# Norm sums behind the attention output and the gated projection: two reduced-precision products in place of one fp32 product

## The reference

```python
for i in range(DEPTH):
    hn = rms_norm(h, norm_mix_pre[i])
    m = deltanet_stickbreak_mixer(hn, ...) if i % 2 == 0 else s5_mixer(hn, ...)
    h = h + rms_norm(m, norm_mix_post[i])
    hn = rms_norm(h, norm_ffn_pre[i])
    f = swiglu_ffn(hn, ffn_w_gate[i], ffn_w_up[i], ffn_w_down[i])
    h = h + rms_norm(f, norm_ffn_post[i])

def rms_norm(x, w):
    return x * lax.rsqrt(jnp.mean(x * x, axis=-1, keepdims=True) + EPS) * w
```

## Time and profile before

| | us |
|---|---|
| median of three runs | 2797.24 |
| lowest, highest | 2795.65, 2801.64 |
| profiled execution | 2792.69 |
| its span, first to last instruction | 2790.9 |
| TensorE matmul busy in it | 2707.2 |
| VectorE busy | 1243.0 |
| GpSimd busy | 1008.4 |
| ScalarE busy | 615.2 |

### The profile page before, as it was taken

One profiled execution on the slowest core, in us unless ns is written; L12 is line 12 of the kernel. 1 busy time (PEld: TensorE's weight loads), 2 busy tenths in 40 slices (PEclk: granted clock), 3 DMA queues, 4 the chain that ended last, 5 costly groups with the idle time before them and its releaser, 6 DMA issues.

```text
span 2790.9 us, 44901 instructions
## 1 busy us (share of the span) xinstructions
PE 2707.2 (97%) x18169; PEld 2577.4 (92%) x18169; DVE 1243.0 (45%) x2137; ACT 615.2 (22%) x1085; POOL 1008.4 (36%) x462
## 2 busy tenths in 40 slices
PE   8999899989999999999999989899999999999997
PEld 7999788867899999999999878799999999999997
DVE  5665566565145444444442446710532322222234
ACT  4231333365241000000000332311410000000002
POOL 6444110033444444444442414152444444444440
PEclk9999999999999999999999999999999999999999
DMA  5236221121231222222222159841331111111102
GB/s 166 93 109 137 84 73 51 58 74 38 70 107 50 78 85 85 85 85 85 85 85 79 51 142 248 246 121 33 106 106 46 45 45 45 45 45 45 46 31 81
DMA packets 158150, 236.51 MB, mean 85 GB/s; under 512 B 57808, under 2 KB 120528, under 8 KB 155856
## 3 DMA queue, kind: packets, MB, share of 16 engines
q1 hardware_dynamic: 53552, 137.11, 16.0%
q10 hardware_dynamic: 104480, 97.71, 12.0%
HBM read 174.89 MB, written 64.09 MB: 86 GB/s over the span
## 4 chain that ended last, share of the span: by engine, by line
issue 37%; PE 36%; POOL 14%; DMA 6%; DVE 3%; ACT 1%; ACTq 1%; SPq 1%; POOLq 0%; DVEq 0%
POOL w_hi L736 9%; PE psum L778 8%; PE psum L779 7%; PE psum L780 7%; POOL w_lo L739 5%; DMA stage<-wstream 5%; PE psum L860 2%; PE psum L1260 2%; DVE area L2291 2%; PE psum L1234 1%; PE psum L1082 1%; PE psum L1103 1%; DVE area L2198 1%; PE psum L1247 1%; DMA area<-s 0%
## 5 line engine op out<-in xcount | busy, mean ns | idle before, releaser
L778 PE MATMUL psum<-x_hi,w_hi 128*128 128x344 f32 (+2 forms) x3456 | 1127.0, 326 | 5.0 <-POOL w_lo L739 3.9
L779 PE MATMUL psum<-x_lo,w_hi 128*128 128x344 f32 (+2 forms) x3456 | 1107.9, 321 | 0.0
L780 PE MATMUL psum<-x_hi,w_lo 128*128 128x344 f32 (+2 forms) x3456 | 1106.5, 320 | 0.0
L736 POOL TENSOR_TENSOR w_hi<-stage,const 128x1024 fp32r<-128x1024 f32 x193 | 478.7, 2480 | 1564.6 <-PE psum L780 1414.0
L778 PEld LDWEIGHTS psum<-x_hi,w_hi 128*128 128x128 f32 x3456 | 651.5, 189 | 16.8 <-POOL w_lo L739 5.4
L779 PEld LDWEIGHTS psum<-x_lo,w_hi 128*128 128x128 f32 x3456 | 651.4, 188 | 3.5 <-issue 1.7
L780 PEld LDWEIGHTS psum<-x_hi,w_lo 128*128 128x128 f32 x3456 | 650.8, 188 | 0.0
L739 POOL TENSOR_TENSOR w_lo<-stage,w_hi 128x1024 fp32r<-128x1024 f32 x193 | 485.3, 2515 | 15.1
L2680 DVE TENSOR_TENSOR area<-area,psum 128x344 f32<-128x344 f32 (+2 forms) x132 | 67.7, 513 | 648.4 <-ACT area L1937 648.4
L778 PE MATMUL psum<-act_hi,w_hi 128*128 128x344 f32 (+2 forms) x1056 | 342.8, 325 | 11.8 <-DVE area L2693 7.3
L780 PE MATMUL psum<-act_hi,w_lo 128*128 128x344 f32 (+2 forms) x1056 | 338.0, 320 | 0.0
(11 more groups left out here) (235 smaller groups left out, 2208.2 us busy)
## 6 DMA issues: line engine op xcount, KB each, us to landing
stage<-wstream SPq DMA_DIRECT2D x193, 512.0 KB, 3.5
s_set<-area ACTq DMA_DIRECT2D x8, 1860.0 KB, 7.8
proj<-area ACTq DMA_DIRECT2D x20, 520.0 KB, 2.7
area<-proj ACTq DMA_DIRECT2D x36, 256.0 KB, 3.7
resid<-area ACTq DMA_DIRECT2D x6, 1376.0 KB, 5.8
area<-resid ACTq DMA_DIRECT2D x6, 1376.0 KB, 10.2
area<-s SPq DMA_DIRECT2D x8, 1024.0 KB, 12.2
area<-s SPq DMA_DIRECT2D x8, 836.0 KB, 10.9
```

What stands on the lines that cost most here:

```text
L736: pool.tensor_tensor(per_block(w_hi[:, slot, :]), src, ones_block, ALU.mult).then_inc(high_split, 1)
L778: mm(out[:, 0:n], w_hi[:, slot, wk], hi[:, xk, a:a + n], start=first, stop=False)
L779: mm(out[:, 0:n], w_hi[:, slot, wk], lo[:, xk, a:a + n], start=False, stop=False)
L780: return mm(out[:, 0:n], w_lo[:, slot, wk], hi[:, xk, a:a + n], start=False, stop=last)
```

## The change

In rounds 1 and 3 a sum is no longer an fp32 product. ScalarE, after squaring a half, waits for the square and copies it, rounded to fp32r, into `x_hi`, in the columns of the cut itself, which no product reads any more. VectorE subtracts that from the square into the same columns of `x_lo` (new function `square_low`). TensorE runs eight fp32r products of a rounded matrix of ones with `x_hi` and eight with `x_lo`, accumulated in the same bank. It waits for each half of either. The ones are rounded once by ScalarE at the start. `square_low` is set into VectorE's list at twelve places.

```diff
+        def split_sums(r):
+            return r in (1, 3)
+        def split_event(r, c, m):
+            return 6 * (r // 2) + 2 * c + m
+        ones_r = sb("ones_r", [P, P], F32R)
...
+                if split_sums(r):
+                    a = cuts_of(r)[c][0]
+                    pe.wait_ge(ones_ready, 1)
+                    for x, done in ((x_hi, nm_sq_high), (x_lo, nm_sq_low)):
+                        for k in range(KT):
+                            if k % 4 == 0:
+                                pe.wait_ge(done, 2 * split_event(r, c, m) + k // 4 + 1)
+                            last = mm(sums[:, 0:n], ones_r[:], x[:, k, a:a + n], start=x is x_hi and k == 0,
+                                      stop=x is x_lo and k == KT - 1)
+                    last.then_inc(nm_sum, 1)
+                    return
...
                     A(sq[half][:, :, 0:n], x[:, ks], ACT.Square).then_inc(nm_square, 1)
+                    if split_sums(r):
+                        act.wait_ge(nm_square, 2 * e + half + 1)
+                        A(x_hi[:, ks, a:a + n], sq[half][:, :, 0:n], ACT.Copy).then_inc(nm_sq_high, 1)
...
             norm_load(0, 0)
             act.wait_ge(eps_ready, 3)
+            act.wait_ge(params_loaded, 32)
+            A(ones_r[:], ones, ACT.Copy).then_inc(ones_ready, 1)
...
+            def square_low(r, c, m):
+                a, n = cuts_of(r)[c]
+                for half in range(2):
+                    ks = slice(4 * half, 4 * half + 4)
+                    dve.wait_ge(nm_sq_high, 2 * split_event(r, c, m) + half + 1)
+                    V.tensor_tensor(x_lo[:, ks, a:a + n], sq_halves[half][:, :, 0:n], x_hi[:, ks, a:a + n].bitcast(F32), sub
+                                    ).then_inc(nm_sq_low, 1)
...
             for c in range(2):
+                square_low(1, c, 0)
                 norm_post(1, c)
+                square_low(1, c, 1)
                 norm_pre(1, c)
                 norm_low(1, c)
+            square_low(1, 2, 0)
...
                 norm_post(r, 2)
                 step(0, 1)
+                square_low(r, 2, 1)
                 step(0, 2)
...
-            glu_product(range(19))
+            glu_product(range(18))
+            square_low(3, 0, 0)
+            glu_product((18,))
             norm_post(3, 0)
             glu_product((19,))
+            square_low(3, 0, 1)
             norm_pre(3, 0)
             glu_product((20,))
             norm_low(3, 0)
+            square_low(3, 1, 0)
             glu_product((21,))
             norm_post(3, 1)
             glu_product((22,))
+            square_low(3, 1, 1)
             norm_pre(3, 1)
             glu_product((23,))
+            square_low(3, 2, 0)
             norm_low(3, 1)
             ffn(1, 3)
```

More of the change, by code:

```diff
@@ L471, in trunk @@
         nm_sum = sem("nm_sum")
+        nm_sq_high = sem("nm_sq_high")
+        nm_sq_low = sem("nm_sq_low")
+        ones_ready = sem("ones_ready")
         nm_stored = [sem(f"nm_stored{i}") for i in range(2)]
```

## The result

The kernel after takes 2812.61 us (2807.96 to 2818.05), the one before, on the same chip, 2795.65 (2793.70 to 2801.64): a ratio of 1.0049 [1.0032, 1.0067], or 13.7 us slower. The direction was right and the size was not.

A forecast was written before the change was run, and what follows sets the result against it. TensorE, busy 97% of the span, was taken as the bound: shorter sums would save 22 us if nothing waited, but late input makes layer 0 +4.2 and layer 1 +3.1, +7.3 on 2797.24, so 2804.5 us; range 2793 to 2810.

The forecast's parts named there:

- sum three: Second cut, first norm: input late beside GpSimd's splits; lasts 5.75 us against 4.36, loss 1.4 in each layer.
- the walk of the lock: VectorE's subtractions and GpSimd's splits wait for each other in turn; in the second cut's first norm, loss 1.4 us.
- Sum one: First cut, first norm: input ready in time, 16 products take 2.56 us instead of 4.46, gain 1.9.
- Sum two: First cut, second norm: input late though GpSimd is idle; lasts 4.6 us against 4.46, loss 0.2.
- Sum four: Second cut, second norm: split, subtraction, split, subtraction; lasts 7.6 us against 4.4, loss 3.2 in each layer.
- rival A: Second cut, second norm, each layer: the other order, loss 1.35 us instead of 3.2; total 2801.8; chance 0.25.
- sum five: Third cut, first norm: 6.8 us instead of 4.4 in layer 0; in layer 1 input is ready, 2.5 us.
- T3 to T5: From the first product behind the fourth sum to that behind the sixth: 37.3 us in layer 0, 35.5 in layer 1.
- B: At the subtractions beside splits, GpSimd doesn't hold VectorE: -4.0 us, total 2793.2; chance 0.14.
- C: At all changed sums, TensorE's own work decides and all input is hidden: -22 us, total 2775; chance 0.04.
- E: The ones product runs at today's rate for each of 16 products: another 4.4 us per sum, over +50; chance 0.03.
- D: Later links in the chains slip too: +12 us, total 2809; chance 0.11.

The follow-up runs named there:

- the first experiment: Against the kernel before, only the first sum of each of the two places is two rounded products, the other ten stay fp32: 2788.24 us, ratio 0.9976.

## Why the prediction was right in direction and short in size

**The step that failed first: sum three.** The prediction took the first square of the second cut at T1 + 7.1 and low parts clear of the splits, as before. It counted the two copies on ScalarE for the evacuations behind them, and left out the store's issue, which stands in the same queue. With it the pre norm starts 1.0 later, the first square at T1 + 7.9 in layer 0 (777.87), and low parts, subtractions and splits meet one after the other. Sum three took 9.25 and 7.18 for 5.75. The run with the store first gave 5.76 and 5.56, and in layer 1, where half clock hardly shifts its start, the first square starts at T1 + 7.0 and the sum ends at T1 + 17.2 (7.1 and 17.35 forecast); so the walk of the lock was right and its starting point was wrong. With the splits held back instead, and the store as late as ever, the sum takes 4.34 and 4.21: it needs both, the late store and the splits, to be as long as it was. The walk should have taken every instruction behind the added ones, the issue of a DMA too, and asked who waits for it.

**The term that was missing: the clock.** The prediction took TensorE's rate as given. Its granted clock fell to half for 6.8 us at sums three, four and five of layer 0 and three and four of layer 1. The products behind sum three take 13.10 instead of 11.60. With the waits filled the places are 8.5 shorter in one pair of traces, 5.7 in the other. No row of before shows this, since TensorE is busy all through the earlier trace rows; but a change that makes TensorE wait could have had it as a rival with a price from a half-clock stretch elsewhere in that trace, which has six, 3.4 to 13.7 long.

**What held.** Sum one 2.59 (2.56 forecast). Sum two 4.71 and 4.40 (4.6). Sum four 7.72 in both layers (7.6): the order split, subtraction, split, subtraction came as drawn from the earlier trace rows, and rival A, the other order, did not occur. (Behind products at half clock TensorE reaches it at T2 + 13.1 and its copies end at T2 + 12.6, both 1.5 later than forecast, so that the duration agrees though the places in time don't.) In layer 1 sum five takes 2.51 (2.5), and T3 to T5 35.94 (35.5). In layer 0 sum five takes 7.14 (6.8) and T3 to T5 39.68, above the 37.3 that the prediction demanded of its own walk; with the waits filled it is 36.5 (806.85 to 843.33), so the walk of VectorE's list was 0.8 too long and the half clock added 3.2.

**The sum again, from the traces.** With the waits filled the places are 5.8 and 3.3 longer than before, 9.1 together: 7.3 as forecast, 4.4 more for sum three (8.73 and 7.15 in that run), less 2.6 that the walk had too long elsewhere. (The products behind sums one to three take 0.2 to 0.3 less than before, six times, 1.5, for the reason given with the first experiment; the third cuts are 0.8 and 0.7 shorter than forecast; sums two and four take 0.4 back.) The half clock makes up the other 8.5 of the 17.6 between the profiled runs. The difference by the ratio, 13.7, is smaller than the 20.0 between the two spans, and so is that of the medians, 17.0: the profiled run of before was 3 us below its median. The walk's excess worked for the forecast by luck: without it the forecast would have been 4.7 us slower, and further from what was measured.

**The rivals.** B (GpSimd doesn't hold VectorE) falls by subtractions at 6.80 and 7.42 the pair. C (TensorE's work alone decides) falls at sum two, which waits 1.49 for a copy with GpSimd idle. E falls with sum one. D, later links slip too, was priced at +12 with another mechanism, further splits ahead of sum five; a slow-down of that size came, but through sum three and the clock, so D is not borne out. The Trainium skill's "SBUF: two separate sides" in "SBUF — State Buffer" states the exclusive lock. The trace agrees in kind, and the held splits show it as cause: without splits beside them the two subtractions of sum three take 1.6 each instead of 7.42 the pair, and the sum 4.34 instead of 9.25.

**The range** ended at 2810 because its worst end was one more split ahead of sum five. It had no room for a cost of another kind.

## What to carry to other kernels

Before a product is made cheaper by giving its input two more steps, look at when the input is ready against when TensorE arrives: here only sums one and five of each place had the slack (five in layer 0 only with VectorE's order changed), and changing these four alone gains 0.27% where changing all twelve loses 0.4 to 0.5%. Walk every queue that an added instruction stands in down to the DMA that it issues, since the wait that decided sum three was for a store issued behind two copies. When a wait is judged by a sum's own time, take the wait ahead of its first instruction too: from one T to the next misses nothing. Work held back from one meeting on the port of VectorE and GpSimd turns up at the next; where TensorE starts to wait in a dense stretch, look at its granted clock behind the wait as well.

## What the runs showed of the hardware

- **Waits are followed by half the clock.** At sums in which TensorE waited 1.2 to 2.9 us at a time, none longer, the granted clock fell to the level of 1.2 GHz for 6.8 us, five times in one run. In the kernel before and in those with waits filled there was none in these places; with one wait of 0.7 (in the run of sums one and five) none either. Sum two of layer 0 waited 1.49 and was not followed by one; with the store first it waited 0.82 and then 1.7, and was. What exactly decides is open.
- **VectorE and GpSimd alternate, instruction by instruction.** Beside back-to-back splits two subtractions of 1.6 us each take 6.8 and 7.4, and each split 3.6 to 3.7 instead of 2.4. At the kernel's start VectorE kept its turn for four. What sets which of the two happens wasn't tried.
- **The spread between runs goes with the clock.** Over 23 runs of the kernel before, on one chip, time falls with the mean granted clock (0.987 to 0.993) at 2.2 us for each 0.001, with a correlation of -0.85; on the two other chips with 17 and 23 runs it is 2.0 and 2.4 us, and -0.87 and -0.90. Differences of 0.1% between two kernels are of the size of what the clock does from run to run.
- **The products behind an fp32 sum start late.** Before, the first gemm product behind a sum is followed by the next after 0.43 us instead of 0.16; behind the new sums it is 0.16.
